# ScalarE as issuer of the projection weights, and a last norm in two VectorE operations with the sample tile first

## The chip, the cores and the metric

The kernel runs on one core of one Trainium2 chip. The core has TensorE (matrix products, here PE), VectorE (DVE), ScalarE (ACT), GpSimd (POOL) and SyncE (SP), each with its own instruction stream, and sixteen DMA engines that SyncE, ScalarE and GpSimd give transfers to. The metric is the device time of one execution in microseconds, lower is better.

## The reference

One inference step of a one-layer decoder for a prompt of 512 rows and 64 sample rows (8 sequences of 8), model width 1024. What matters for the change is the conditioning, the first projection and the last norm:

```python
mod = (jax.nn.silu(c) @ w_ada + b_ada).reshape(B, 6, 1, D_MODEL)
shift1, scale1, gate1, shift2, scale2, gate2 = [mod[:, i] for i in range(6)]
h = x * (1 + scale1) + shift1
proj = h @ w_in                       # 1024 -> 3072: qa, ka, va, qb, kb, vb
...                                   # two kinds of attention, w_o, a first layer norm, ConvFFN up
y = (jax.nn.gelu(a, approximate=False) * g) @ w_down + b_down
x = layer_norm(DEEPNORM_ALPHA * x + gate2 * y, ln2_g, ln2_b)   # (x - mu) * rsqrt(var + EPS) * g + b
```

The step also returns updated window buffers (`win_k_sample`, `win_v_sample`): old cache rows copied from one place of the chip's memory to another, and new rows behind them.

## The kernel before

**First projections.** Work goes in 30 units, numbered n = 5 s + t: section s (0 to 5) is a chunk of 512 columns of `w_in`, t is the row tile (0 to 3 the prompt, t = 4 = TP the sample rows). Every product is made of three float32r products (high by high, high by rest, rest by high; lines 1723 to 1725; for the sample rows of most sections two, lines 1718 and 1719). At the end of a section VectorE and GpSimd split the next chunk into high and rest (lines 1177 to 1180 and 774). Between the units TensorE also makes the later modulation: `ada_rows(ch)` (line 1666) multiplies chunk ch of `w_ada`, which lies in the one buffer `late`, and `ada_sum(ch)` (line 1679) follows one unit later. `LATE_UNIT = {4: 3, 5: 6, 6: 10, 7: 13, 8: 16, 9: 20, 10: 23, 11: 26}` says before which unit: chunk 7 before unit 13, chunk 9 before unit 20. Chunk ch + 1 can be loaded only when the rows of chunk ch are done (`ada_mm`), since both use `late`.

**Who issues what.** Before the change SyncE issues everything in this stage from one list in the order of the units: the stores of projected rows (lines 604 to 625, each behind a wait for the rows), the loads of the next `w_in` chunk (line 544, 2 MB, behind `w_used`), the loads of `late` (line 582, 2 MB, behind `ada_mm`), and the copies of window caches (line 586, `move_window`, 4 MB from memory to memory, at the units of `COPY_UNIT`). A wait for one holds up all that stands behind it. ScalarE copies value rows out of PSUM (line 910) and turned queries (line 916).

**The end.** The down projection has two halves of 512 columns. Half 1 first takes the gated rows f = 0 to 11 for all five tiles, then for one tile after another the last ten, f = 12 to 21: 30 matmuls for a prompt tile, 20 for the sample tile. `split_gated(z)` on VectorE (lines 1533 to 1535) makes the high and rest parts that these read. When a tile is complete VectorE runs `add_half(1, t)` (gate, residual, statistics: lines 1574 to 1578, for the sample tile also 1571 and 1572) and the norm: mean and variance (1626, 1627), a root on ScalarE (1079), reciprocal and factor (1631, 1632), the scaling x * r - mean * r on ScalarE (1074), the product with the norm's weights on VectorE (`weight_norm`, 1620), the addition of its bias on GpSimd (853; for the sample tile on VectorE, 1638), then the store (728, 731). The order of the tiles is 0, 1, 2, 3, TP.

## Time and profile before

| | us |
|---|---|
| median of 3 runs | 1175.63 |
| lowest and highest of them | 1174.1, 1181.54 |
| the profiled execution, its own time | 1176.66 |
| its span in the trace | 1175.0 |
| TensorE busy | 1023.7 (87%) |
| VectorE busy | 827.1 (70%) |

The span is the time from the first to the last record of the trace; the execution's own time is 1.66 us more. The first projections with their modulation lie between 40 and 270 us of the span, attention between 270 and 610, the up projection between 708 and 1060, the down projection and the last norm behind it.

### The profile page before, as it was taken

What the parts mean: (1) busy time and instruction counts of PE and PEld (TensorE: products, weight loads), DVE (VectorE), ACT (ScalarE), POOL (GpSimd) and SP (SyncE); (2) the same over time, 40 slices, a digit from 0 to 9 for tenths busy, and PEclk for the clock granted to TensorE, in tenths of its full rate; (3) what the DMA queues carried; (4) which work ended last, traced back from release to release, by engine and by line L of the source; (5) the groups of instructions that cost most, each with busy time, mean ns of one, the idle gap of its engine ahead of it and who ended that gap; (6) DMA issues with size and microseconds to landing.
All of it is one profiled execution on the core that took longest, in us unless ns stands there. A gap on an engine that the chain in (4) does not pass through costs nothing.

```text
span 1175.0 us, 23900 instructions
## 1 busy us (share of the span) xinstructions
PE 1023.7 (87%) x9297; PEld 832.1 (71%) x9297; DVE 827.1 (70%) x1545; ACT 270.8 (23%) x600; POOL 450.5 (38%) x575
## 2 busy tenths in 40 slices
PE   4599989995788888888888969999999999998994
PEld 2377657673566666566676759999999999776873
DVE  1637545644886877888876784676676767999978
ACT  0300000001343433343352032323232323000001
POOL 0423223214243444434406034565566656333323
PEclk8699999998898989898998988999999999999998
DMA  8948799978899999999963151677676622414102
GB/s 299 410 157 312 269 351 365 318 246 266 289 365 368 327 337 368 349 331 331 337 253 127 42 190 47 219 255 277 248 253 250 215 73 75 155 60 147 53 2 80
DMA packets 101030, 276.54 MB, mean 235 GB/s; under 512 B 9608, under 2 KB 33174, under 8 KB 97317
## 3 DMA queue, kind: packets, MB, share of 16 engines
q1 hardware_dynamic: 85701, 223.56, 54.2%
q0 software_dynamic: 15168, 51.39, 12.6%
q8 instruction: 74, 1.21, 0.4%
q14 instruction: 39, 0.32, 0.1%
q10 hardware_dynamic: 48, 0.05, 0.0%
HBM read 264.60 MB, written 76.69 MB: 290 GB/s over the span
## 4 chain that ended last, share of the span: by engine, by line
PE 53%; DVE 16%; issue 15%; DMA 6%; POOL 5%; SPq 2%; POOLq 2%; ACT 1%; ACTq 0%; DVEq 0%; PEldq 0%
PE wide L1723 15%; PE wide L1724 14%; PE wide L1725 14%; DMA ring<-in_w_ada 2%; DVE ring_r L1180 2%; POOLq L480 1%; PE wide L1666 1%; POOL room L509 1%; DVE ht_r L1533 1%; DMA room<-in_w_ada 1%; DVE ring L1260 1%; POOL x_sb L509 1%; POOL x_sb L805 1%; PE wide L1807 1%; DVE ring_r L1179 1%
## 5 line engine op out<-in xcount | busy, mean ns | idle before, releaser
L828 POOL TENSOR_TENSOR ring_r<-ring,ring_r 128x1024 fp32r<-128x1024 f32 x70 | 180.8, 2592 | 232.3 <-DVE ring_r L1139 201.1
L1723 PE MATMUL wide<-x_sb_r,ring_r 128*128 128x288 f32 x704 | 211.1, 300 | 11.4 <-DVE ht_r L1162 8.4
L1724 PE MATMUL wide<-ht_r,ring_r 128*128 128x288 f32 x704 | 209.3, 297 | 0.0
L1725 PE MATMUL wide<-x_sb_r,ring_r 128*128 128x288 f32 x704 | 208.7, 297 | 0.0
L1723 PEld LDWEIGHTS wide<-x_sb_r,ring_r 128*128 128x128 f32 x704 | 133.4, 190 | 14.3 <-issue 14.3
L1260 DVE STREAM_TRANSPOSE ring<-ring 128x512 f32<-128x512 f32 x208 | 129.0, 677 | 12.0 <-DMA ring<-in_cache_k 10.3
L1725 PEld LDWEIGHTS wide<-x_sb_r,ring_r 128*128 128x128 f32 x704 | 134.2, 191 | 0.0
L1724 PEld LDWEIGHTS wide<-ht_r,ring_r 128*128 128x128 f32 x704 | 133.8, 190 | 0.0
L1723 PE MATMUL wide<-ring_r,x_sb_r 128*128 128x512 f32 (+1 forms) x208 | 87.0, 418 | 11.9 <-DVE ht_r L1162 8.7
L1725 PE MATMUL wide<-ring_r,ht_r 128*128 128x512 f32 x216 | 87.2, 404 | 0.0
L1724 PE MATMUL wide<-ring_r,x_sb_r 128*128 128x512 f32 (+1 forms) x208 | 83.7, 402 | 0.0
L1548 DVE SCALAR_TENSOR_TENSOR room<-room,vec_t 128x512 f32<-128x512 f32 x44 | 55.4, 1260 | 40.0 <-ACT room L1056 40.0
L1048 ACT ACTIVATE room<-wide,vec_t 128x576 f32<-128x576 f32 x44 | 32.8, 744 | 207.1 <-PE wide L1725 202.3
L1725 PE MATMUL wide<-ring_r,room_r 128*128 128x512 f32 x192 | 77.5, 404 | 0.0
L1550 DVE SCALAR_TENSOR_TENSOR room<-room,vec_t 128x512 f32<-128x512 f32 x44 | 73.5, 1671 | 1.6
L774 POOL TENSOR_TENSOR ring_r<-ring,ring_r 128x512 fp32r<-128x512 f32 x24 | 33.5, 1401 | 88.1 <-ACT ring_r L876 44.1
L1139 DVE CAST ring_r<-ring 128x1024 fp32r<-128x1024 f32 x62 | 41.9, 687 | 34.0 <-DMA ring<-in_w_up 32.1
L1807 PE MATMUL wide<-room 128*128 128x128 f32 x320 | 53.9, 303 | 12.0 <-ACT room L950 8.6
L1723 PEld LDWEIGHTS wide<-ring_r,x_sb_r 128*128 128x128 f32 (+1 forms) x208 | 39.9, 192 | 32.6 <-issue 16.7
L517 POOL DMA_DIRECT2D x_sb<-in_cache_v x60 | 33.0, 550 | 72.5 <-issue 71.4
L1723 PE MATMUL wide<-ring_r,ht_r 128*128 128x512 f32 x136 | 55.8, 410 | 5.0 <-DVE room L1574 2.9
L1807 PEld LDWEIGHTS wide<-room 128*128 128x128 f32 x320 | 44.1, 205 | 22.1 <-ACT room L950 12.8
(271 smaller groups left out, 2119.4 us busy)
## 6 DMA issues: line engine op xcount, KB each, us to landing
ring<-in_cache_k SPq DMA_DIRECT2D x128, 256.0 KB
out_wks<-in_cache_win_k SPq DMA_DIRECT2D x8, 4080.0 KB, 19.5
out_wvs<-in_cache_win_v SPq DMA_DIRECT2D x8, 4080.0 KB, 19.3
ring<-in_w_up SPq DMA_DIRECT2D x22, 1024.0 KB, 7.6
room<-in_w_ada SPq DMA_DIRECT2D x8, 2048.0 KB, 9.7
ring<-in_cache_win_k SPq DMA_DIRECT2D x16, 1024.0 KB
x_sb<-in_cache_v POOLq DMA_DIRECT2D x60, 256.0 KB, 5.4
room<-in_cache_v POOLq DMA_DIRECT2D x56, 256.0 KB, 5.3
```

Of the source, the lines that this page charges most:

```text
L517: eng.dma_start(home[t:P:4, :, :], flat_v[1][bass.ds(pg, 1)].rearrange("a (i m) h d -> m (a i) (h d)", i=4))\
L774: nc.gpsimd.tensor_tensor(rest, w, high.bitcast(F32), ALU.subtract).then_inc(win_pool, 1)
L828: nc.gpsimd.tensor_tensor(rest, w, high.bitcast(F32), ALU.subtract).then_inc(wl_rest, 1)
L1048: nc.scalar.activation(u_b[:, k % 2, 2:2 + NT].rearrange("p (h t) -> p h t", h=2), pair, ACT.Identity, bias=vec_t[:, 0, 48 + f:49 + f]).th ...
L1139: nc.vector.tensor_copy(pair_of(n, slice(k, k + 2))[0], slot(SLOT_OF[n])[:, k:k + 2, :]).then_inc(wl_high, 1)
L1260: last = nc.vector.transpose(ktg[:, G % NK, :, 32 * t:32 * t + 32], kraw[G % NK][:, t, :].rearrange("p (g d) -> p g d", d=32))
L1548: then(nc.vector.scalar_tensor_tensor(out=c_p, in0=u_b[:, k % 2, 1:1 + SEQ], scalar=tap(1), in1=c_p, op0=ALU.mult, op1=ALU.add))
L1550: nc.vector.scalar_tensor_tensor(out=c_p, in0=u_b[:, k % 2, 0:SEQ], scalar=tap(0), in1=c_p, op0=ALU.mult, op1=ALU.add)
L1723: nc.tensor.matmul(out, left[0], right[0], start=first, stop=False)
L1724: nc.tensor.matmul(out, left[0], right[1], start=False, stop=False)
L1725: return nc.tensor.matmul(out, left[1], right[0], start=False, stop=last)
L1807: last = nc.tensor.matmul(bank[:, 0:P], pt_b[:, u % 2, P * kb:P * kb + P], vp[:, kb, m, P * (n // 2):P * (n // 2) + P], start=(kb == 0), s ...
```

## The change

1. The function `load_late` moves out of SyncE's part and takes the issuing engine. SyncE still issues chunk 4; chunks 5 to 11 and the `w_in` chunks of sections 2 to 5 are now issued by ScalarE, from its own job list, at positions `at + 0.3` and `n + 0.4` between its copies. The waits in front of them are the same. SyncE keeps stores and window copies.
2. The last norm is two VectorE operations over the whole tile: (x - mean) * weights, which needs no root and runs while ScalarE makes it, and then (that) * r + bias. ScalarE keeps the root alone; GpSimd has no part in it.
3. In half 1 of the down projection the last ten f of the sample tile come first: `END_TILES = [TP, 0, 1, 2, 3]`. VectorE, ScalarE and the stores follow that order.

```diff
+        END_TILES = [TP, 0, 1, 2, 3]
...
+        def load_late(eng, ch):
+            if ch > 4:
+                eng.wait_ge(ada_mm, ch)
+            src = a["w_ada"][0].rearrange("(k p) n -> p k n", p=P)
+            eng.dma_start(late, src[:, :, CH * ch:CH * ch + CH]).then_inc(late_in, 16)
...
@@ SyncE, at the end of each unit
-                if t == TP:
-                    if s < 4:
-                        load_chunk(6 + s)
-                for ch, at in LATE_UNIT.items():
-                    if at == n and ch < 11:
-                        load_late(ch + 1)
...
@@ ScalarE, the projections
+            jobs += [(at + 0.3, "late", ch + 1) for ch, at in LATE_UNIT.items() if ch < 11]
+            jobs += [(n + 0.4, "w_in", 2 + s) for n, (s, t) in enumerate(units) if t == TP and s < 4]
             for _, what, n in sorted(jobs):
+                if what == "late":
+                    load_late(act, n)
+                    continue
+                if what == "w_in":
+                    c = CHUNK_AT[("in", n)]
+                    act.wait_ge(w_used, chunk_before(c) + 1)
+                    act.dma_start(slot(SLOT_OF[c]), src_in[:, :, CH * n:CH * n + CH]).then_inc(w_in_slot[SLOT_OF[c]], 16)
+                    continue
...
@@ ScalarE, the last norm
-                nc.scalar.activation(x, x, ACT.Identity, bias=mv2[0:rows, t, 4:5], scale=mv2[0:rows, t, 3:4]).then_inc(n2_scaled, 1)
...
@@ GpSimd
-            for t in range(TP):
-                pool.wait_ge(n2_w, t + 1)
-                nc.gpsimd.tensor_tensor(x_sb[:, t, :], x_sb[:, t, :], ln2[:, 2, :], ALU.add).then_inc(y_out, 1)
...
@@ VectorE, the last norm
-            for t in range(TP + 1):
+            for i, t in enumerate(END_TILES):
                 add_half(1, t)
...
                 nc.vector.tensor_scalar(v[:, 1:2], v[:, 1:2], EPS, None, ALU.add).then_inc(n2_var, 1)
-                if 0 < t < TP:
-                    weight_norm(t - 1)
-                dve.wait_ge(n2_rt, t + 1)
+                nc.vector.scalar_tensor_tensor(out=x, in0=x, scalar=v[:, 0:1], in1=ln2[0:rows, 1, :],
+                                               op0=ALU.subtract, op1=ALU.mult)
+                dve.wait_ge(n2_rt, i + 1)
                 then(nc.vector.reciprocal(v[:, 3:4], v[:, 2:3]))
-                nc.vector.scalar_tensor_tensor(out=v[:, 4:5], in0=v[:, 0:1], scalar=-1.0, in1=v[:, 3:4],
-                                               op0=ALU.mult, op1=ALU.mult).then_inc(n2_fac, 1)
+                nc.vector.scalar_tensor_tensor(out=x, in0=x, scalar=v[:, 3:4], in1=ln2[0:rows, 2, :],
+                                               op0=ALU.mult, op1=ALU.add).then_inc(y_out, 1)
...
@@ TensorE, half 1 of the down projection
-                    steps += [(f, t) for t in range(TP + 1) for f in range(TAIL, FT)]
+                    steps += [(f, t) for t in END_TILES for f in range(TAIL, FT)]
```

On SyncE, from the first window copy of the projections on (`out_wks` and `out_wvs` behind `<-in_cache_win` are the copies, `in_w_ada` the loads of `late`), before:

```order
L586 DMA out_wks<-in_cache_win_k 64x16320
L582 DMA room<-in_w_ada 128x8x512 [waits ada_product]
L544 DMA ring<-in_w_in 128x8x512 [waits w_used]
L586 DMA out_wvs<-in_cache_win_v 64x16320
L604 DMA out_wkp<-mix 128x512 [waits rope_done] x2
L582 DMA room<-in_w_ada 128x8x512 [waits ada_product]
L604 DMA out_wkp<-mix 128x512 [waits rope_done] x2
L586 DMA out_wks<-in_cache_win_k 64x16320
L608 DMA out_wks<-ring 8x512 [waits rope_done]
L608 DMA out_wks<-ring 8x512 x7
L544 DMA ring<-in_w_in 128x8x512 [waits w_used]
L619 DMA out_wvp<-room 128x512 [waits proj_taken_act]
```

And with the change, from the same copy on:

```order
L585 DMA out_wks<-in_cache_win_k 64x16320
L585 DMA out_wvs<-in_cache_win_v 64x16320
L603 DMA out_wkp<-mix 128x512 [waits rope_done] x4
L585 DMA out_wks<-in_cache_win_k 64x16320
L607 DMA out_wks<-ring 8x512 [waits rope_done]
L607 DMA out_wks<-ring 8x512 x7
L618 DMA out_wvp<-room 128x512 [waits proj_taken_act] x2
```

The loads are gone from between the stores, and two copies stand next to each other (the same happens at the third pair, units 14 and 18).

On ScalarE, from the first turned queries (unit 0) to the first transfers of attention, before:

```order
L916 ACTIVATE room<-wide 128x4x128 [waits qk_transposed] x4
L910 ACTIVATE room<-wide 128x512 [waits proj_product] x4
L910 ACTIVATE ring<-wide 64x512 [waits proj_product]
L916 ACTIVATE room<-wide 128x4x128 [waits qk_transposed] x4
L910 ACTIVATE room<-wide 128x512 [waits proj_product] x4
L910 ACTIVATE ring<-wide 64x512 [waits proj_product]
```

And with the change, the first part of the same stretch (to unit 14):

```order
L915 ACTIVATE room<-wide 128x4x128 [waits qk_transposed]
L526 DMA room<-in_w_ada 128x8x512 [waits ada_product]
L915 ACTIVATE room<-wide 128x4x128 [waits qk_transposed]
L902 DMA ring<-in_w_in 128x8x512 [waits w_used]
L915 ACTIVATE room<-wide 128x4x128 [waits qk_transposed] x2
L526 DMA room<-in_w_ada 128x8x512 [waits ada_product]
L902 DMA ring<-in_w_in 128x8x512 [waits w_used]
L909 ACTIVATE room<-wide 128x512 [waits proj_product]
L526 DMA room<-in_w_ada 128x8x512 [waits ada_product]
L909 ACTIVATE room<-wide 128x512 [waits proj_product] x3
L526 DMA room<-in_w_ada 128x8x512 [waits ada_product]
L909 ACTIVATE ring<-wide 64x512 [waits proj_product]
```

Chunk 7 is the `in_w_ada` row between the first value copy (unit 10) and the next three.

On VectorE, the last tile of the program, before (the sample tile, with the weights of tile 3 and the bias behind it):

```order
L1571 COPY room<-wide 64x512 [waits down_product]
L1572 TENSOR_TENSOR room<-room,wide 64x512 [waits dve_seq]
L1574 TENSOR_TENSOR room<-room,mix 64x512 [waits dve_seq]
L1577 TENSOR_TENSOR x_sb<-x_sb,room 64x512 [waits down_taken]
L1578 BN_STATS stat<-x_sb 64x6 [waits dve_seq]
L1626 BN_AGGR mv<-stat 64x2 [waits dve_seq]
L1627 TENSOR_SCALAR mv<-mv 64x1 [waits dve_seq]
L1631 RECIPROCAL mv<-mv 64x1 [waits norm2_root]
L1632 SCALAR_TENSOR_TENSOR mv<-mv 64x1 [waits dve_seq]
L1620 TENSOR_TENSOR x_sb<-x_sb,room 128x1024 [waits norm2_scaled]
L1620 TENSOR_TENSOR x_sb<-x_sb,room 64x1024 [waits norm2_scaled]
L1638 TENSOR_TENSOR x_sb<-x_sb,room 64x1024 [waits norm2_weighted]
```

And with the change (prompt tile 3 is now the last):

```order
L1567 TENSOR_TENSOR room<-wide,mix 128x512 [waits down_product]
L1570 TENSOR_TENSOR x_sb<-x_sb,room 128x512 [waits down_taken]
L1571 BN_STATS stat<-x_sb 128x6 [waits dve_seq]
L1613 BN_AGGR mv<-stat 128x2 [waits dve_seq]
L1614 TENSOR_SCALAR mv<-mv 128x1 [waits dve_seq]
L1615 SCALAR_TENSOR_TENSOR x_sb<-x_sb,mv,room 128x1024
L1618 RECIPROCAL mv<-mv 128x1 [waits norm2_root]
L1619 SCALAR_TENSOR_TENSOR x_sb<-x_sb,mv,room 128x1024 [waits dve_seq]
```

Twelve instructions behind the last product have become eight, and no wait for ScalarE's scaling is among them.

## Rows read from the trace of the kernel before

**Rows 1.** The page: busy us, share of the span, instructions, of TensorE.

```profile
PE 1023.7 (87%) x9297; PEld 832.1 (71%) x9297; DVE 827.1 (70%) x1545; ACT 270.8 (23%) x600; POOL 450.5 (38%) x575
```

**Rows 2.** Timeline of TensorE, 117 to 200 us: start, us, engine, line, operation, [idle before].

```profile
122.76 1.90 PE L1666 MATMUL wide<-room,c_t 128*9 128x512 f32 x16
...
150.58 3.18 PE L1666 MATMUL wide<-room,c_t 128*9 128x512 f32 x16 [3.65 <-DMA room<-in_w_ada]
153.69 0.80 PE L1723 MATMUL wide<-ring_r,x_sb_r 128*128 128x512 f32 x1
...
197.48 1.90 PE L1666 MATMUL wide<-room,c_t 128*9 128x512 f32 x16
```

**Rows 3.** Timeline of the transfers that SyncE issues, 10 to 292 us.

```profile
120.77 0.52 SPq L586 DMA_DIRECT2D out_wks<-in_cache_win_k  x1
...
136.67 0.41 SPq L544 DMA_DIRECT2D ring<-in_w_in  x1
...
137.74 0.43 SPq L582 DMA_DIRECT2D room<-in_w_ada  x1
...
174.42 0.40 SPq L582 DMA_DIRECT2D room<-in_w_ada  x1
174.86 10.52 SPq L586 DMA_DIRECT2D out_wvs<-in_cache_win_v  x1
```

**Rows 4.** Transfers issued at 120.8, 137.7 and 174 to 175: KB, us to landing.

```profile
out_wks<-in_cache_win_k SPq DMA_DIRECT2D x1, 4080.0 KB, 15.4
...
room<-in_w_ada SPq DMA_DIRECT2D x1, 2048.0 KB, 12.8
...
out_wvs<-in_cache_win_v SPq DMA_DIRECT2D x1, 4080.0 KB, 32.0
room<-in_w_ada SPq DMA_DIRECT2D x1, 2048.0 KB, 21.0
```

**Rows 5.** Timeline of ScalarE: the value copy of unit 10, and turned queries later.

```profile
130.96 0.60 ACT L910 ACTIVATE room<-wide 128x512 f32<-128x512 f32 x1 [33.08 <-PE wide L1725]
...
186.89 0.60 ACT L916 ACTIVATE room<-wide 128x512 f32<-128x512 f32 x1 [20.10 <-PE wide L1783]
```

**Rows 6.** Two stretches: us, busy us by engine, granted clock, DMA share, GB/s.

```profile
70.00:80.00 10.00, 10.00 (x55) 6.98 (x54) 3.40 (x7) 0.60 (x1) 2.57 (x2) 1.00 0.11 19
150.00:160.00 10.00, 9.42 (x45) 5.68 (x45) 0.69 (x1) 0.17 (x1) 0.00 (x0) 0.83 1.19 431
```

**Rows 7.** Timeline of TensorE and VectorE in half 1 of the down projection.

```profile
1129.30 0.50 PE L1723 MATMUL wide<-ring_r,room_r 128*128 128x512 f32 x1 [2.43 <-DVE room_r L1535]
...
1134.06 0.43 PE L1725 MATMUL wide<-ring_r,room_r 128*128 128x512 f32 x1
...
1132.25 0.69 DVE L1535 TENSOR_TENSOR room_r<-room,room_r 128x512 fp32r<-128x512 f32 x1
...
1159.16 0.40 PE L1719 MATMUL wide<-ring_r,room_r 128*64 128x512 f32 x1
```

**Rows 8.** Timeline of VectorE behind the last prompt tile, to the end.

```profile
1154.97 0.69 DVE L1574 TENSOR_TENSOR room<-wide,mix 128x512 f32<-128x512 f32 x1 [0.60 <-PE wide L1725]
...
1157.46 1.22 DVE L1620 TENSOR_TENSOR x_sb<-x_sb,room 128x1024 f32<-128x1024 f32 x1
1158.59 0.16 DVE L1631 RECIPROCAL mv<-mv 128x1 f32<-128x1 f32 x1
1158.78 2.34 DVE L1632 SCALAR_TENSOR_TENSOR mv<-mv 128x1 f32<-128x1 f32 x1
...
1170.40 1.22 DVE L1638 TENSOR_TENSOR x_sb<-x_sb,room 64x1024 f32<-64x1024 f32 x1
```

**Rows 9.** Line 1511, a scalar-tensor-tensor over a tile: ns min/median/max, first and last start.

```profile
L1511 DVE SCALAR_TENSOR_TENSOR x_sb<-x_sb,room x5: 1207/1215/1216, 641.3 to 688.9; 128x1024 f32<-128x1024 f32 x4, 64x1024 f32<-64x1024 f32 x1
```

**Rows 10.** The last stores: issue on SyncE, and KB and us to landing.

```profile
1171.65 0.53 SPq L731 DMA_DIRECT2D out_ys<-x_sb  x1
...
out_yp<-x_sb SPq DMA_DIRECT2D x4, 512.0 KB, 2.6
```

More of the change, by code:

```diff
@@ L380, in build @@
         g_used = sem("gated_used")
-        n2_var, n2_rt, n2_fac = sem("norm2_variance"), sem("norm2_root"), sem("norm2_factors")
-        n2_scaled, n2_w = sem("norm2_scaled"), sem("norm2_weighted")
-        y_last = sem("y_sample_ready")
+        n2_var, n2_rt = sem("norm2_variance"), sem("norm2_root")
         st_done = sem("sample_tile_of_h2")
@@ L574, in _ @@
             sp.dma_start(pages[:, :], a["page_table"].rearrange("b n -> (b n)").rearrange("(o n) -> o n", o=1)).then_inc(page_in, 16)
-            def load_late(ch):
-                if ch > 4:
-                    sp.wait_ge(ada_mm, ch)
-                src = a["w_ada"][0].rearrange("(k p) n -> p k n", p=P)
-                sp.dma_start(late, src[:, :, CH * ch:CH * ch + CH]).then_inc(late_in, 16)
             def move_window(i, names=(("cache_win_k", "wks"), ("cache_win_v", "wvs"))):
@@ L590, in flat @@
                 return ap.rearrange("t h d -> t (h d)")
-            load_late(4)
+            load_late(sp, 4)
             n_rope = n_v = 0
@@ L903, in _ @@
                     jobs.append((n + 2.5, "q", n))
+            jobs += [(at + 0.3, "late", ch + 1) for ch, at in LATE_UNIT.items() if ch < 11]
+            jobs += [(n + 0.4, "w_in", 2 + s) for n, (s, t) in enumerate(units) if t == TP and s < 4]
+            src_in = a["w_in"][0].rearrange("(k p) n -> p k n", p=P)
             for _, what, n in sorted(jobs):
+                if what == "late":
[6 more added lines that the diff above has]
+                    continue
                 s, t = units[n]
@@ L1068, in _ @@
                 nc.scalar.activation(conv_out(i), bk(6 + i % 2)[0:18, :], ACT.Copy).then_inc(us_a, 1)
-            def scale_norm(t):
+            for i, t in enumerate(END_TILES):
                 rows = P if t < TP else NS
-                act.wait_ge(n2_fac, t + 1)
-                x = x_sb[0:rows, t, :]
-                nc.scalar.activation(x, x, ACT.Identity, bias=mv2[0:rows, t, 4:5], scale=mv2[0:rows, t, 3:4]).then_inc(n2_scaled, 1)
-            for t in range(TP + 1):
-                rows = P if t < TP else NS
-                act.wait_ge(n2_var, t + 1)
+                act.wait_ge(n2_var, i + 1)
                 nc.scalar.activation(mv2[0:rows, t, 2:3], mv2[0:rows, t, 1:2], ACT.Sqrt).then_inc(n2_rt, 1)
-                scale_norm(t)
         @block.vector
@@ L1567, in add_half @@
                 j = (TP + 1) * half + t
-                dve.wait_ge(dn_mm, j + 1)
+                done = (TP + 1) * half + (END_TILES.index(t) if half else t) + 1
+                dve.wait_ge(dn_mm, done)
                 src = bk(j % 8)[0:rows]
@@ L1574, in add_half @@
                 nc.vector.tensor_tensor(y3[0:rows], src, gate2[0:rows, kind, cols], ALU.mult).then_inc(dn_d, 1)
-                dve.wait_ge(dn_d, j + 1)
+                dve.wait_ge(dn_d, done)
                 x = x_sb[0:rows, t, cols]
@@ L1614, in _ @@
                     add_half(0, z - FT - NG_BUF + 2)
-            def weight_norm(t):
-                rows = P if t < TP else NS
-                x = x_sb[0:rows, t, :]
-                dve.wait_ge(n2_scaled, t + 1)
-                nc.vector.tensor_tensor(x, x, ln2[0:rows, 1, :], ALU.mult).then_inc(n2_w, 1)
-            for t in range(TP + 1):
+            for i, t in enumerate(END_TILES):
                 rows = P if t < TP else NS
@@ L2103, in _ @@
                     z, j = FT * half + f, (TP + 1) * half + t
-                    if t == 0:
+                    if t == (END_TILES[0] if half and f >= TAIL else 0):
                         if half == 0 and f == 10:
```

9 lines of the change are left out of this document (2 added, 7 removed).

## The prediction

> **What bounds the kernel now.** I read the page first: TensorE is busy for 1023.7 us of a span of 1175.0 [rows 1]. So a change elsewhere can pay only where TensorE waits, or in front of its first and behind its last matmul. This change touches two such places.
>
> The first is the projections. I listed TensorE's idle times in its timeline from 60 to 270 us. There is one wait of over 2 us: 3.65 us in front of the rows of chunk 7, released by the DMA of `in_w_ada` [rows 2]. SyncE's list shows why that load is late [rows 3]. It is issued at 137.74, though its condition (rows of chunk 6 done, begun at 122.76 [rows 2]) held at about 124.6. In front of it stand the window stores, which wait for the rotary rows of unit 9, and the load of the `w_in` chunk of section 3, issued at 136.67. It lands after 12.8 us, at 150.5 [rows 4], and TensorE starts at 150.58. The other waits of this stretch are under 2 us, and none is for a DMA. The short ones belong to VectorE's and GpSimd's splits and stay.
>
> The second is the end. The last matmul starts at 1159.16 and takes 0.40 [rows 7], so 15.4 us follow to the end of the span. In them VectorE finishes tile 3's norm, does the sample tile, the two `weight_norm` and the bias, to 1171.62 [rows 8], and the last store takes the rest [rows 10]. Among those operations is one of a single column (line 1632) that took 2.34 us [rows 8], while GpSimd added a bias in the same time.
>
> **The projections, part by part.** ScalarE issues chunk 7 behind its value copy of unit 10, which runs from 130.96 to 131.56 [rows 5]. That is about 131.6 in place of 137.74, 6.1 us earlier. The `w_in` chunk of section 3 waits for the product of unit 9, which TensorE finishes just before the rows of chunk 6 at 122.76 [rows 2], so it goes 14 us earlier, from 136.67 [rows 3] to about 122.6. Chunk 7 now shares the DMA engines with the end of the window copy of 120.77, which took 15.4 us to land [rows 4], and with that `w_in` chunk. Where it lands is bounded from both sides. With its 12.8 us of before [rows 4], when it had the `w_in` chunk in front of it too, it lands at 144.4. In the worst case the copy is served first (to 136.2), and then both chunks in the 13.9 us from 136.67 to 150.5 [rows 3, 4], which gives 150.1. TensorE needs it at 150.58 - 3.65 = 146.9. The worst case puts all of `w_in` behind the copy, although it is issued only 1.8 us after it and has 9 us alone with it, so I take the first: the wait goes, whole.
>
> What goes with it is read in the rows: 3.65 us of wait; the sixteen matmul records behind it took 3.18 us, where the same sixteen took 1.90 at 122.76, so 1.28 more: from 150 to 160 us the granted clock was 0.83 of full speed [rows 6], part of it at 1.2 GHz in place of 2.4, right behind the idle time; and the next one took 0.80 [rows 2], about 0.3 more than after a full-speed group. Sum 3.65 + 1.28 + 0.3 = 5.2 us. Bounds: 0.5 (worst landing) and 5.2.
>
> The other six late loads move by little, since their condition sets them: chunk 5 with the rows of chunk 4, chunk 8 behind the value copy of unit 13, as before. The issue itself costs ScalarE about 0.4 us each by SyncE's rows [rows 3], eleven times, beside 23% busy [rows 1]: on no path. What the waits in front of them hold up are ScalarE's copies of the next unit, which come later than the condition anyway. SyncE, freed of its waits, sends two copies close together twice. The first pair goes out at about 50 us, in front of a stretch in which the DMA engines had little to do (share 0.11 from 70 to 80 us [rows 6]) and nothing waits for a load. The second goes out behind unit 14, and that is the place to watch (first rival).
>
> Attention starts with loads issued behind the last value copy, so it moves up whole. Nothing in it has a fixed time, so I carry the 5.2 us to the end.
>
> **The end, part by part.** TensorE gets later. The splits of f = 18 to 21 are what it waits for in the first of the five tiles (2.43 us idle at 1129.30); the last one is done at 1132.94 [rows 7]. Before, prompt tile 0 stood there with 30 matmuls, ending at 1134.3. Now the sample tile stands there with two matmuls per f: the last pair starts at 1133.0 and issues in 0.86 at the half clock (0.43 each at 1134.06 [rows 7]), to 1133.9. Behind it come 120 matmuls of prompt tiles in place of 90 and the sample tile's 20, at 0.228 apiece (110 from 1134.06 to 1159.16 [rows 7], so 6.8 us per tile). The last starts at 1133.9 + 119 x 0.228 = 1161.0 and ends at 1161.4, where it was 1159.56: 1.8 us later. If the half clock lasts 3 us longer, because TensorE has less to do under the splits, 1.5 more.
>
> VectorE: from the end of a prompt tile to the start of the first big operation it takes 1157.46 - 1154.97 = 2.49 us [rows 8]. The two big ones are not in this trace in this form. Nearest above and below in kind are line 1511, a scalar-tensor-tensor over 128x1024, at 1.215 us [rows 9], and line 1620, a tensor-tensor of that size, at 1.22 [rows 8]; with a pointer to a column as scalar I see no reason for more or less, and take 1.22 each (bounds 1.2 and 1.4). The reciprocal begins 1.13 behind the first, the second 0.19 behind that [rows 8]. The root on ScalarE is done within the first. Sum per prompt tile: 2.49 + 1.13 + 0.19 + 1.22 = 5.0 us, under the 6.8 that TensorE needs per tile. So VectorE waits for TensorE at each, and only one tile's 5.0 stands behind the last matmul. The sample tile needs about 6.4 us (two more operations of 0.7), from 1133.9 to 1140.3, just before tile 0 at 1140.7.
>
> The end is then 1161.4 + 5.0 + the store. The sample store took 1175.0 - 1171.65 = 3.35 from issue to the end; a prompt tile's store lands after 2.6 [rows 10], so between 2.6 and 3.35, and I take 3.25, since it is the last one's case. With 0.04 to VectorE's start, 1161.4 + 0.04 + 5.03 + 3.25 = 1169.7 in place of 1175.0: gain 5.3 us, bounds 3.5 (long half clock, dearer operations) and 6.0 (landing 2.6).
>
> **Sum.** 5.2 + 5.3 = 10.5 us. The profiled execution's own time was 1176.66, which gives 1166.2. It lay 1.03 above the median of 1175.63, which gives 1165.1. I predict 1165.
>
> **Rivals.** *Copies crowd out the loads.* Chunk 9 landed at 174.42 + 21.0 = 195.4 [rows 3, 4], with only 2.1 us to spare before its rows at 197.48 [rows 2]. Now it is on another engine's queue beside two window copies; the second was issued at 174.86 and landed 32.0 later, at 206.9 [rows 3, 4]. If a load of small rows is served behind copies of large ones, it lands when they do. All of this moves 5.2 earlier: the deadline to 192.3 and the second copy's landing to 201.7 at the latest, so the wait is up to 9.4 us, and I take about half, 5. For it: the thin margin. Against it: chunk 9 is 2 MB, and if the engines give each queue half of their time it is through before either copy, since it then needs no more than twice the 5 to 6 us that 2 MB take alone (chunk 7 landed 13.9 us behind the issue of 4 MB). With 5 us of wait and 1.5 of half clock (1.28 + 0.3 above) the projections' gain is gone: 1165.0 + 6.5 = 1171.5.
>
> By the Trainium skill ("DMA: Bandwidth & Descriptors", "Queues, rings and completion order") each DMA engine goes round-robin between the queues of SyncE and ScalarE, packet by packet; by that the load is not starved, unless a copy's packets are much the larger. No row of before has a copy beside ScalarE's loads, so the trace is silent on it.
>
> *The load lands no earlier.* The DMA engines move the same bytes, and if chunk 7 comes at 150.1 as in the worst case above, 0.5 of the 5.2 remains: 1169.7. For it: copy, `w_in` and chunk 7 are 8 MB from 120.8 on. The Trainium skill ("DMA: Bandwidth & Descriptors", "Issuing engines are not separate DMA queues") says that issuing from several engines saves only the time of issue, which speaks for this one; the row of the wait shows that here the time of issue is the point, since the load stood 13 us behind its condition.
>
> *Slower than before.* Starvation at every load: if those before units 13, 16, 20, 23 and 26 each came late by as much as chunk 7 does now, each would cost 5.2. It decides from the third such wait: none gained, two more lost, 1175.63 - 5.3 + 10.4 = 1180.7. Against it: only chunk 9 has a copy on both sides, and ScalarE's queue copies have slack (one of them waits 20.10 us at 186.89 [rows 5]).
>
> **Chances.** Forecast, 1162.5 to 1167.5: 0.62. Crowding, 1168 to 1173: 0.20. Lands no earlier, 1167.5 to 1170.5: 0.09. Slower, about 1180: 0.03. More than forecast, since clock and splits fall otherwise: 0.06. The range 1161.5 to 1172 leaves out 0.03 below, the slower case and part of the crowding. One per cent of this time, 11.8 us, is about what a measurement can tell: 1163.9 is the border. The forecast lies just above it; a third of its chance and the larger gain fall below: faster 0.26, same 0.71, slower 0.03.
>
> **What would show it.** Right: no wait of TensorE for `in_w_ada` at unit 13, chunk 7 issued near 131.6, unit 13's rows near 147; chunk 9's rows without a wait; the end of attention 5 us earlier. In the tail the last matmul about 1.8 us later against the end of the splits, two VectorE operations of 1.2 us per tile, 8.3 us between the last matmul and the end. Wrong: a wait before unit 20, big operations of 2 us or more, or a half clock that lasts into tile 1.

## The result: slower, by two waits of TensorE for late loads

| | before | after |
|---|---|---|
| median of 20 runs each, us | 1174.63 | 1186.86 |
| lowest and highest | 1167.53, 1181.54 | 1171.48, 1194.21 |
| the profiled execution, its own time | 1176.66 | 1189.11 |
| its span | 1175.0 | 1187.4 |

The ratio is 1.0066, 95% interval 1.0043 to 1.009. It leaves out runs over 1.5% above the fastest of their kernel, as a disturbed run would be; the times after spread more widely than that by themselves, so that the medians, 12.2 us or 1.0% apart, say it better. The twenty times fall in two groups: four from 1171.5 to 1176.9 and sixteen from 1181.2 to 1194.2. The profiled execution is of the second group.

In the kernel after, matmul lines 1723 to 1725 are 1705 to 1707, the late load is line 526, the load of `w_in` 902, a window copy 585 and `ada_rows` 1648. The first view is what TensorE waits for from 40 to 285 us. The columns are the line that waits, its releaser, us in total, times, and the longest.

```profile
PE wide L1648 <- DMA room<-in_w_ada: 21.9, 2, 14.2
```

TensorE's timeline shows where these two stand (start, us, engine, line, [idle before]). They answer to the wait of 3.65 us in [rows 2].

```profile
161.63 3.60 PE L1648 MATMUL wide<-room,c_t 128*9 128x512 f32 x16 [14.16 <-DMA room<-in_w_ada]
...
217.07 3.60 PE L1648 MATMUL wide<-room,c_t 128*9 128x512 f32 x16 [7.78 <-DMA room<-in_w_ada]
```

The first is unit 13 (chunk 7), the second unit 20 (chunk 9). Now the two queues side by side. ScalarE's timeline, its DMA issues:

```profile
122.55 0.37 ACTq L902 DMA_DIRECT2D ring<-in_w_in  x1
...
131.51 0.38 ACTq L526 DMA_DIRECT2D room<-in_w_ada  x1
...
178.16 0.37 ACTq L902 DMA_DIRECT2D ring<-in_w_in  x1
...
186.13 0.37 ACTq L526 DMA_DIRECT2D room<-in_w_ada  x1
```

SyncE's timeline, the copies:

```profile
121.30 0.52 SPq L585 DMA_DIRECT2D out_wks<-in_cache_win_k  x1
143.09 0.52 SPq L585 DMA_DIRECT2D out_wvs<-in_cache_win_v  x1
181.61 0.52 SPq L585 DMA_DIRECT2D out_wks<-in_cache_win_k  x1
182.17 0.59 SPq L585 DMA_DIRECT2D out_wvs<-in_cache_win_v  x1
```

Chunk 7 and the `w_in` chunk of section 3 are issued when I said they would be, 131.5 and 122.6. But the view of the DMA gives 30.1 us from issue to landing for chunk 7, in place of 12.8 [rows 4], and 21.4 for the `w_in` chunk ahead of it:

```profile
ring<-in_w_in ACTq DMA_DIRECT2D x1, 2048.0 KB, 21.4
...
room<-in_w_ada ACTq DMA_DIRECT2D x1, 2048.0 KB, 30.1
```

What the engines did in the meantime is in the rows by queue (q1 is SyncE's, q10 ScalarE's; packets, MB, share of sixteen engines, which passes 100% where the times of packets overlap). From 123 to 130 us, copy of 121.30 and `w_in` together:

```profile
q1 hardware_dynamic: 32, 2.09, 87.2%
q10 hardware_dynamic: 16, 0.03, 1.6%
```

From 148 to 157 us, copy of 143.09 and chunk 7; and from 186.5 to 198 us, the copies of 181.61 and 182.17 and the two loads of 178.16 and 186.13, which land after 33.3 and 30.9 us:

```profile
q1 hardware_dynamic: 52, 3.26, 99.0%
q10 hardware_dynamic: 44, 0.09, 2.6%
...
q1 hardware_dynamic: 80, 4.18, 102.7%
q10 hardware_dynamic: 71, 0.14, 3.5%
```

And from 211 to 217 us, when both copies are through:

```profile
q10 hardware_dynamic: 1134, 2.29, 103.3%
```

A packet of a load is about 2 KB, one of a copy 65 KB (2.09 MB in 32; of the 80 packets of 186.5 to 198 us, 65 are of over 8 KB). The engines go between the queues in packets, so beside a copy a load gets about a thirtieth of the bytes, as 2 KB are of 65; alone it moves 2 MB in under 6 us. So each 4 MB copy takes nearly all of the engines and the load waits for its end. That is the chain: `w_in` waits for the copy of 121.30 (landed at 137.1) and lands at 144.0; chunk 7 comes behind it in ScalarE's queue; and just then, at 143.09, SyncE sends the next copy, which lands 17.2 us later. Its packets fill the engines from about 147.5 us on. By 148 chunk 7 has all but 0.25 of its 2.1 MB, and for this last eighth it needs until 161.6. In the kernel before, that copy was issued after chunk 7 on the same queue, and so could not pass it.

The Trainium skill says ("DMA: Bandwidth & Descriptors", "Queues, rings and completion order") that each engine goes round-robin between the queues packet by packet. The trace agrees where both queues have work for the whole stretch: 52 packets to 44 from 148 to 157 us, and 80 to 71 from 186.5 to 198. The first stretch, with 32 to 16, begins before the load's packets do; from 128 to 134 us it is 32 to 32.

The projections end later by this. A good mark is the first load of window keys for attention on SyncE, at 270.02 before and at 287.32 after: 17.3 us. The two waits are 21.94 us against 3.65 before, 18.3 more. From the mark to the end it is 1187.4 - 287.3 = 900.1 us against 905.0.

The end itself came out nearly as drawn up. VectorE's timeline, the last prompt tile's norm, answers to [rows 8]:

```profile
1181.69 1.27 DVE L1615 SCALAR_TENSOR_TENSOR x_sb<-x_sb,mv,room 128x1024 f32<-128x1024 f32 x1
1182.89 0.15 DVE L1618 RECIPROCAL mv<-mv 128x1 f32<-128x1 f32 x1
1183.08 1.28 DVE L1619 SCALAR_TENSOR_TENSOR x_sb<-x_sb,mv,room 128x1024 f32<-128x1024 f32 x1
```

The last matmul starts at 1178.77 and ends at 1179.16, 8.2 us ahead of the end of the span. The place that answers to the head of [rows 7] is, in TensorE's timeline:

```profile
1145.95 0.67 PE L1700 MATMUL wide<-ring_r,room_r 128*128 128x512 f32 x1 [3.12 <-DVE room_r L1527]
```

From there to the end of the span it is 41.4 us; before it was 1175.0 - 1129.3 = 45.7. One part is not as drawn up. The last matmul starts 32.8 us behind that row (1178.77 - 1145.95), where it was 29.9 (1159.16 - 1129.30), so it is 3.0 us later and not 1.8.

### The profile page after: what moved, and what is told of

It reads as the page before. It is cut to its first block, busy times and chain, and to the rows that moved or that the text cites. A ratio compares the mean times of both kernels' runs of the same rounds, so it can differ in the third digit from the quotient of the medians.

```text
span 1187.4 us, 23890 instructions
## 1 busy us (share of the span) xinstructions
PE 1025.9 (86%) x9297; PEld 831.9 (70%) x9297; DVE 819.1 (69%) x1544; ACT 264.5 (22%) x595; POOL 442.6 (37%) x571
## 2 busy tenths in 40 slices
DMA packets 101030, 276.54 MB, mean 233 GB/s; under 512 B 9608, under 2 KB 33174, under 8 KB 97317
## 4 chain that ended last, share of the span: by engine, by line
PE 47%; DVE 19%; issue 15%; DMA 9%; POOL 5%; POOLq 2%; SPq 1%; ACT 1%; ACTq 0%; DVEq 0%; PEldq 0%
PE wide L1705 13%; PE wide L1706 13%; PE wide L1707 13%; DMA room<-in_w_ada 5%; DVE ht_r L1525 2%; DMA ring<-in_w_ada 2%; PE wide L1648 2%; DVE ring_r L1172 2%; POOLq L479 2%; DVE ht_r L1526 1%; DVE room_r L1527 1%; POOL room L508 1%; PE wide L1845 1%; DVE x_sb L1601 1%; DVE ring_r L1131 1%
## 5 line engine op out<-in xcount | busy, mean ns | idle before, releaser
L1705 PE MATMUL wide<-ring_r,x_sb_r 128*128 128x512 f32 (+1 forms) x208 | 86.9, 418 | 13.6 <-DVE ht_r L1154 10.6
L1707 PE MATMUL wide<-ring_r,ht_r 128*128 128x512 f32 x216 | 86.7, 401 | 0.0
L1540 DVE SCALAR_TENSOR_TENSOR room<-room,vec_t 128x512 f32<-128x512 f32 x44 | 52.6, 1196 | 42.0 <-ACT room L1055 42.0
L1542 DVE SCALAR_TENSOR_TENSOR room<-room,vec_t 128x512 f32<-128x512 f32 x44 | 73.5, 1671 | 1.6
L1131 DVE CAST ring_r<-ring 128x1024 fp32r<-128x1024 f32 x62 | 42.0, 688 | 32.8 <-DMA ring<-in_w_up 31.0
L1845 PE MATMUL wide<-ring,x_sb 128*32 128x128 f32 (+1 forms) x1792 | 59.8, 279 | 3.2 <-DVE ring L1252 2.7
```

Of the source, the lines that this page charges most:

```text
L1131: nc.vector.tensor_copy(pair_of(n, slice(k, k + 2))[0], slot(SLOT_OF[n])[:, k:k + 2, :]).then_inc(wl_high, 1)
L1540: then(nc.vector.scalar_tensor_tensor(out=c_p, in0=u_b[:, k % 2, 1:1 + SEQ], scalar=tap(1), in1=c_p, op0=ALU.mult, op1=ALU.add))
L1542: nc.vector.scalar_tensor_tensor(out=c_p, in0=u_b[:, k % 2, 0:SEQ], scalar=tap(0), in1=c_p, op0=ALU.mult, op1=ALU.add)
L1705: nc.tensor.matmul(out, left[0], right[0], start=first, stop=False)
L1707: return nc.tensor.matmul(out, left[1], right[0], start=False, stop=last)
L1845: last = nc.tensor.matmul(bank[32 * nn:32 * nn + 32, at:at + nk], qbd[:, w % 2, g].rearrange("p i q -> p (i q)"), keys[:, g, 0:nk], start= ...
```

## Experiments

Twelve kernels were run, 4 to 12 times each, and each beside the kernel before on the same chip. As between the kernels above, single profiles differ by several us from attention on, so the verdicts rest on the ratios of repeated runs and on where waits stand. I call the mark of the last section (the first load of window keys) "the mark"; it is 270.0 before and 287.3 after. Chunk 4, loaded ahead of anything that the experiments move, is issued between 45.7 and 48.9 us, so marks that differ by 1 or 2 us say little.

My theory (A): the loss is all in the projections, because loads of small rows on one queue meet copies of large rows on the other; the end gains what it was to gain.

### 1. Each half of the change alone

`tail_only` has the new norm and order of tiles and all loads on SyncE as before. `issue_only` has the loads on ScalarE and the norm of before.

> The second and third part of the change alone (two VectorE operations for the last norm, the sample tile first); SyncE issues all loads as before. If the loss of the whole change lies in the projections, this one gains: from the end of the splits to the end of the span 37.8 us as in the changed kernel, in place of 42.1, so about 4.3 us faster than before, near 1170. If the tail has a part in the loss, this one is no faster than 1174.

> The first part of the change alone: ScalarE issues the loads of the first projections, the last norm as before. Theory (window copies crowd out the loads on ScalarE's queue): TensorE waits for chunks 7 and 9, as in the changed kernel by 14 and 8 us in place of 3.65, so 15 to 17 us slower than before where it falls as it did in the profiled execution, about 1188 to 1192, with a wide spread. Rival (the loss comes with the tail): about 1170.

| | median | ratio, 95% interval |
|---|---|---|
| tail_only | 1172.82 | 0.9956 (0.9934 to 0.9977) |
| issue_only | 1191.69 | 1.0137 (1.0081 to 1.0193) |

The end gains 0.44% of 1177.6, 5.2 us. The issue by ScalarE loses over 1%, in the range expected. The profiled execution of `issue_only` was the fastest of its four (1179.91, the others 1190.7 to 1198.3), and shows how narrow the edge between the two groups of times probably is. There the `w_in` chunk landed at 142.9, chunk 7 began, and the copy of unit 11 was issued at 144.19, 1.3 us behind the landing: chunk 7 landed after 17.8 us and TensorE waited 0.26. In the profile of the change the copy was issued 0.9 us ahead of the landing (143.09 and 144.0), and the wait was 14.16. These are two profiles, one of each kernel; what the other executions did at this place no trace shows. Unit 20 waited all the same, in TensorE's timeline of `issue_only`:

```profile
202.16 3.42 PE L1671 MATMUL wide<-room,c_t 128*9 128x512 f32 x16 [7.96 <-DMA room<-in_w_ada]
```

### 2. Small rows in the copies

`small_rows` is the changed kernel, but each of the eight copies of the projections goes as two transfers, of the even and of the odd rows of 2 KB.

```diff
-                    sp.dma_start(o[dst][0, i, 0:PAST - DS], a[name][0, i, DS:PAST]).then_inc(copied, 16)
+                    if i < 4:
+                        for odd in range(2):
+                            sp.dma_start(o[dst][0, i, odd:PAST - DS:2], a[name][0, i, DS + odd:PAST:2]).then_inc(copied, 16)
```

> The changed kernel, but the eight window copies of the projections go as even and odd rows of 2 KB each, the same bytes in the same places of SyncE's list. Theory A (a DMA engine takes one descriptor of each queue in turn, so a copy with descriptors of up to 65 KB gets nearly all of the time beside rows of 2 KB): the loads now get about half, chunk 7 lands before 147 us and chunk 9 before 192, no wait, 1163 to 1167. Theory B (SyncE's queue goes first, or the bandwidth is simply not there): waits as in the changed kernel, near 1187.

Measured: 1170.6 us, ratio 0.9929 (0.9898 to 0.9959). One wait for `in_w_ada` is left at unit 13, where I had expected none (chunk 7 lands at 148.1), and none at unit 20:

```profile
148.14 1.91 PE L1652 MATMUL wide<-room,c_t 128*9 128x512 f32 x16 [2.79 <-DMA room<-in_w_ada]
```

The DMA by queue from 123 to 137 us, copy beside `w_in`:

```profile
q1 hardware_dynamic: 1427, 2.89, 56.6%
q10 hardware_dynamic: 1175, 2.38, 46.3%
```

With packets of one size the two queues share nearly evenly; from 125 to 135 us, when both are busy throughout, it is 913 packets to 942 and 1.84 MB to 1.93. The same bytes move, the same engines issue them at the same places, and what was 1% slower is 0.7% faster. The size of the packets is the cause, and theory B is out. The mark is at 266.0. Beside the end alone (`tail_only`, 0.9956) the gain is small, and the intervals overlap: the early loads still share the engines with the copies.

### 3. Without the copies

`no_copies` leaves out the eight window copies of the projections (their rows of the output are not written).

> The changed kernel without the eight window copies of the projections (33 MB, those output rows are left out; the other eight stay). Theory A and B alike (the loads wait because of the copies): each load lands in 7 to 9 us, no wait for in_w_ada, about 1163 to 1165. Rival C (a load issued by ScalarE is slow by itself, or its issue is late): waits before units 13 and 20 stay at several us.

Measured: 1166.81 us, ratio 0.9908 (0.9878 to 0.9939). No wait for the late loads is left, and those that ScalarE issues land in 7.8 to 9.0 us, one, issued 2.7 us behind a `w_in` chunk, in 10.6. The mark is at 266.4. Rival C, that ScalarE's issue is slow by itself, is out.

`no_copy_11` leaves out only the copy of 143.09 (its rows of the output are not written).

```diff
+                    if i == 1 and dst == "wvs":
+                        sp.sem_inc(copied, 16)
+                        continue
```

> The changed kernel without one of its copies: the window copy of unit 11 (the second sample's values) is left out, so that part of wvs is not written. Theory A (that copy, issued at 143.09, took chunk 7's bandwidth): chunk 7 lands at 142 to 150, PE waits 0 to 3 us for it in place of 14.2, and the two groups of times (1171 to 1177, and 1181 to 1194) become one; the wait of unit 20 (7.8 us) stays; the time is 1172 to 1177 us, a ratio of 0.995 to 1.0. Rival D (the w_in load ahead of it on its own queue holds chunk 7 back): the wait stays above 8 us and the time above 1181 us.

Measured: 1174.83 us, ratio 0.9989 (0.9964 to 1.0014). Nine of its ten times lie between 1170.5 and 1176.9, one is 1182.4. Chunk 7 landed after 17.9 us, at 149.0, and TensorE waited 1.96 us for it and 8.7 at unit 20. So this one copy makes the slow group, and rival D, under which the `w_in` chunk was enough, is out.

### 4. The queues exchanged

`copies_on_act` leaves the loads with SyncE and gives ScalarE the copies.

```diff
+            jobs += [(n + 0.35, "copy", n) for n in COPY_UNIT]
...
+                if what == "copy":
+                    i, which = COPY_UNIT[n]
+                    name, dst = ("cache_win_k", "wks") if which == "k" else ("cache_win_v", "wvs")
+                    act.wait_ge(pj_mm, n + 1)
+                    act.dma_start(o[dst][0, i, 0:PAST - DS], a[name][0, i, DS:PAST]).then_inc(copied, 16)
```

> The two queues are exchanged: the late loads and the w_in loads stay on SyncE's queue as before, and the eight window copies of the projections are issued by ScalarE, each behind the matmuls of the unit at which it stood. The last norm is that of the changed kernel. Theory A (the DMA engines take the two queues by turns, one packet each, and a packet of a 4 MB copy is ten times longer and more than one of a load): it doesn't matter which engine issues what, and the loads starve as in the changed kernel: chunk 7, issued at about 137.7, lands at 155 to 165, and PE waits 8 to 16 us for it; the time is 1180 us or more, a ratio of 1.005 to 1.02. Rival B (SyncE's queue is served ahead of ScalarE's): the loads land as fast as they do alone, in 8 to 13 us, there is no wait above 4 us, and the time is that of the tail change alone or less, 1165 to 1173 us, a ratio of 0.990 to 0.996.

Measured: 1199.64 us, ratio 1.0244 (1.0184 to 1.0304). The waits, in TensorE's timeline:

```profile
163.22 3.60 PE L1647 MATMUL wide<-room,c_t 128*9 128x512 f32 x16 [13.99 <-DMA room<-in_w_ada]
...
268.50 3.60 PE L1647 MATMUL wide<-room,c_t 128*9 128x512 f32 x16 [11.00 <-DMA room<-in_w_ada]
```

and the DMA by queue from 148 to 158 us, with the copy, now in q10, fully under way:

```profile
q10 hardware_dynamic: 48, 3.13, 87.0%
q1 hardware_dynamic: 48, 0.10, 2.6%
```

Rival B is out: neither queue goes first. It is the copy that wins, whoever issues it, and the turns are one packet for one, 48 to 48. (A stretch that begins earlier hides this: from 146 to 148 us the load, still almost alone, moves 348 packets.) The mark is at 297.5. The time is above the range that I gave. Of the 10 us between the marks the waits for `in_w_ada` make 3.1 (25.0 us in all). The rest is in TensorE's own busy time: 213.8 us from 40 to 298 in place of 206.0 from 40 to 287, for nearly the same number of matmul records (988 and 985), with a granted clock of 0.88 in place of 0.90.

### 5. One queue, loads ahead of the stores

`sp_early` has SyncE issue everything, with each load ahead of the stores of its unit, and one copy a unit later.

```diff
-COPY_UNIT = {..., 8: (1, "k"), ...}
+COPY_UNIT = {..., 9: (1, "k"), ...}
...
+                if t == TP and s < 4:
+                    load_chunk(6 + s)
+                for ch, at in LATE_UNIT.items():
+                    if at == n + 1 and ch < 11:
+                        load_late(ch + 1)
                 kb_rows = slice(P * t, P * t + P)
```

> One queue, but the loads ahead: SyncE issues everything, as before, but each w_in and late load is issued ahead of the stores of its unit, and not behind them, and the copy of unit 8 stands one unit later. The last norm is that of the changed kernel. Theory A (what costs is two queues with packets of such unequal size, and the early issue is worth its full wait where the queue is one): the wait of 3.7 us for chunk 7 becomes 0 to 1.5 us, unit 20 doesn't wait, and the time is 1163 to 1170 us, a ratio of 0.988 to 0.994. Rival C (an early load always meets a copy, on either queue): the copy ahead of it in the queue delays chunk 7 as much as the issue gains, the wait stays at 3 to 5 us, and the time is that of the tail change alone, about 1172 us, a ratio of 0.995 to 0.998.

Measured: 1174.29 us, ratio 0.9981 (0.9958 to 1.0004), no better than the end alone (0.9956). My expectation of 1163 to 1170 was missed, and the DMA rows say why. Chunk 7 is issued at 125.36 and lands after 11.7 us, so unit 13 waits for nothing. But the copies of 137.34 and 143.22 now go out together, and chunk 8, issued at 149.49, stands behind them and lands after 24.2 us:

```profile
173.75 3.60 PE L1642 MATMUL wide<-room,c_t 128*9 128x512 f32 x16 [5.87 <-DMA room<-in_w_ada]
```

The rival C of this run was right in what it said of an early load, one load later than I put it. These copies and loads landed in the order of their issue, and with 8 MB in front of it the load took 24.2 us, where 7.8 to 9.0 were enough in `no_copies`.

### 6. The copies moved to the second half

`late_copies_act` is the changed kernel with its eight copies moved out of the projections. `late_copies_sp` is the same with the loads on SyncE as before.

```diff
-                if n in COPY_UNIT:
-                    i, which = COPY_UNIT[n]
-                    move_window(i, (("cache_win_k", "wks") if which == "k" else ("cache_win_v", "wvs"),))
...
+            move_window(0)
             load_chunk(FIRST_LATE + 13)
+            move_window(1, (("cache_win_k", "wks"),))
...
             for n in range(FIRST_LATE + 17, len(CHUNKS)):
                 load_chunk(n)
+                if n == FIRST_LATE + 17:
+                    move_window(1, (("cache_win_v", "wvs"),))
+                    move_window(2)
+                elif n == FIRST_LATE + 18:
+                    move_window(3)
```

> The changed kernel, with nothing left out, but its eight window copies of the projections are issued by SyncE in the second half of the program: three around the load of 944 to 971 us, three behind the load of 1077, two behind the load of 1110, where the page's rows show the DMA engines idle for over half of the time. Theory A (the copies beside the early loads are the whole loss, and the early issue is worth 3.7 to 4 us once they are gone): no wait for in_w_ada is above 1 us, the projections end 3.5 to 4 us earlier than in the kernel before, and the time is 1164 to 1169 us, a ratio of 0.989 to 0.993, near that of the kernel without these copies (0.9908). Rival E (the copies meet later loads or stores just as badly): a new wait of 3 us or more for in_w_up, in_w_down or the spilled rows after 900 us, and a ratio of 0.994 or more.

> The same move of the copies, but with the loads issued by SyncE behind the stores as in the kernel before (the last norm is that of the changed kernel). It tells what the issue by ScalarE is worth by itself once no copy is near. Chunk 7 is then issued at about 137.7 and lands 8 to 9 us later, at about 146.5, so that its wait is 0 to 1 us in place of 3.7: if so, the time is within 1.5 us of that of the other kernel with late copies, 0.989 to 0.994, and ScalarE's queue isn't needed at all. If the issue by ScalarE is worth more than that, this kernel is 3 us or more behind the other.

| | median | ratio, 95% interval | the mark | wait at unit 13 |
|---|---|---|---|---|
| late_copies_act | 1179.35 | 1.0033 (1.0014 to 1.0053) | 264.2 | none |
| late_copies_sp | 1184.61 | 1.0066 (1.0041 to 1.0092) | 270.9 | 3.85 |

Two things follow. First, the early issue is worth what the prediction put on it: with no copy near, the kernel with ScalarE's issue is 5.3 us faster by the medians (the means are 5.1 apart, 95% interval about 2 to 8). Its mark is 6.7 us earlier, of which 1.3 was there at the issue of chunk 4 (46.48 against 47.83), so 5.4 are of the projections. My expectation that SyncE's issue would do as well was wrong. It is late by its place behind the stores and behind the `w_in` chunk: `w_in` goes at 137.43, chunk 7 at 138.50, and it lands after 13.0 us even without a copy.

Second, rival E holds for this placement, by my own fault. TensorE's timeline of `late_copies_act` has, in place of 1.80 and 2.43 us in the kernel before:

```profile
1000.13 0.80 PE L1710 MATMUL wide<-ring_r,ht_r 128*128 128x512 f32 x1 [6.76 <-DVE ht_r L1532]
...
1131.17 0.77 PE L1705 MATMUL wide<-ring_r,room_r 128*128 128x512 f32 x1 [5.63 <-POOL ring_r L825]
```

The second is plain: SyncE's list has three copies behind the load of 1077.76, and the last load of `w_down` at 1110.95; it landed after 16.6 us, against 6.8 before, and GpSimd began its split at 1128.31, 16.78 us idle. The first comes about in the same way: the chunk of `w_down` issued at 965.93, behind two copies and with one right after it, lands after 13.7 us, against 8.1 before, and VectorE, which splits it, waits 7.68 us for it at 979.70, against 1.15. The DMA engines looked idle on the page because the next load was not due yet, and a copy that takes them 11 us fits such a gap only if nothing stands behind it. The same two waits stand in `late_copies_sp` (6.25 and 6.05 us), so the comparison of the two is fair.

### 7. The norm and the order apart

`norm_only` is `tail_only` with the sample tile last, as before. `order_only` is the kernel before with the sample tile first.

> The kernel before with the two-operation last norm, but the sample tile last in its part as before. If the gain of the end is all from the norm (the sample tile's place worth nothing): 1169 to 1174 us, a ratio of 0.993 to 0.998, as with the whole change of the end (0.9956). If the sample tile's place gives a part, as I reckoned (the last tile, one of 128 rows, has a longer store but the sample tile's fixed wait for its matmuls is earlier): about 1175 us, a ratio of 0.998 to 1.0.

> The kernel before with its last norm on three engines as it is, but the sample tile first in its part. Beside the kernel with the two-operation norm alone (0.9946), which left the order, it splits the end's gain of about 5 us. By my reckoning of the prediction the order is worth little: the last tile is then a full one, with a store of 2.6 us, as the tile before it had: a ratio of 0.997 to 1.001. If the order carries the gain: 0.993 to 0.996.

| | median | ratio, 95% interval | first wait of half 1's last part to the end, us |
|---|---|---|---|
| norm_only | 1167.84 | 0.9946 (0.9923 to 0.9968) | 1166.1 - 1125.5 = 40.6 |
| order_only | 1177.27 | 1.0010 (0.9992 to 1.0027) | 1179.3 - 1131.6 = 47.7 |
| tail_only | 1172.82 | 0.9956 (0.9934 to 0.9977) | 1177.0 - 1135.6 = 41.4 |
| before | | | 1175.0 - 1129.3 = 45.7 |

The norm is the whole gain, and no gain of the order shows: by the last column, which is of single profiles, the order costs 0.8 us with the new norm and 2.0 with the old. It leaves TensorE the sample tile's few matmuls, where the splits set the pace, with the long tiles still to come. From the end of the last split to the start of the last matmul it is 26.2 us before and 26.1 in `norm_only`, but 29.2 to 29.6 in `tail_only`, `order_only` and the changed kernel, which have the sample tile first. The ratios alone can't tell what the order costs; the intervals overlap.

### 8. Two copies moved to where no load follows

`two_late` is the changed kernel with the two copies of units 11 and 18 behind the last load of `w_down`.

```diff
-COPY_UNIT = {..., 8: (1, "k"), 11: (1, "v"), 14: (2, "k"), 18: (2, "v"), ...}
+COPY_UNIT = {..., 8: (1, "k"), 14: (2, "k"), ...}
...
             for n in range(FIRST_LATE + 17, len(CHUNKS)):
                 load_chunk(n)
+            for i in (1, 2):
+                move_window(i, (("cache_win_v", "wvs"),))
```

> The changed kernel, nothing left out, with two of the eight window copies of the projections (those of units 11 and 18, which stand beside chunks 7 and 9) issued by SyncE behind the last load of w_down, at about 1105 to 1110 us, where nothing is loaded any more. Unlike the kernel with eight late copies no load stands behind them. Theory A (only a copy in the way of a load costs): the waits for in_w_ada are 0 to 3 us at unit 13 and 0 to 2 us at unit 20, the last w_down chunk lands in 4 to 9 us (16.6 behind three copies), VectorE's and GpSimd's splits of it wait for nothing new, and the time is 1166 to 1171 us, a ratio of 0.991 to 0.996, which beats both kernels and comes near that of small rows (0.9929). Rival F (8 MB of copies beside the end of the down projection and its stores costs by itself, for instance by the chunk's own landing): the end from the last issue of w_down on is 3 us or more longer than in the changed kernel, and the ratio is 0.997 or more.

Measured: 1166.79 us, ratio 0.9916 (0.9888 to 0.9943), faster than the kernel before and than the changed one with nothing left out, and within the error of the kernel without copies. It can't be told apart from `norm_only` (0.9946), which has SyncE issue everything: the intervals overlap. Unit 13's wait is 1.69 us, unit 20 has none, the last `w_down` chunk lands after 7.0:

```profile
150.89 1.90 PE L1650 MATMUL wide<-room,c_t 128*9 128x512 f32 x16 [1.69 <-DMA room<-in_w_ada]
...
1129.20 0.50 PE L1702 MATMUL wide<-ring_r,room_r 128*128 128x512 f32 x1 [3.12 <-DVE room_r L1529]
```

From the second row to the end it is 41.9 us, half a microsecond more than in the changed kernel, so rival F, in which copies beside the end cost 3 us or more, is out.

## Why the prediction was wrong

**The sign was wrong**, and the range did not hold the time: 1165 (1161.5 to 1172) against 1186.86. The term for the end nearly held, the one for the projections did not.

- *When the loads are issued.* "About 131.6" and "about 122.6": 131.51 and 122.55. Right.
- *Where chunk 7 lands.* This is the step that failed. I bounded it between 144.4 and 150.1 and took 144.4, at which the whole wait of 3.65 us goes; it landed at 161.6, and the wait was 14.16. The worst case had the copy of 120.77 served first, then both loads. It lacked the copy of unit 11. Before, that copy stands on SyncE's queue at 142.5, behind the load of 137.74, and can't pass it; I listed what chunk 7 would be moved past on SyncE's list, but not what would now be beside it in the time in which it moves its bytes. Taking that copy away brings the wait from 14.16 to 1.96 us, with chunk 7 at 149.0: inside my bounds, but near the worst one, so that even then the value that I took was wrong.
- *How the engines share.* I argued for my value that `w_in` has 9 us alone with the copy of 120.77, and against crowding that the load "is through before either copy", "if the engines give each queue half of their time". They give turns in packets, one for one, and in bytes that was 2.09 MB to 0.03 in seven of the 9 us on which I built. The sentence on the Trainium skill had the right rule with its exception, "unless a copy's packets are much the larger", and then called the trace silent on it; but that some packets are large could have been read from the page of the kernel before, which counts 101030 packets, of them 97317 under 8 KB. With equal packets the forecast's mechanism works in part: the wait falls to 2.79 us, not to nothing (0.9929).
- *What the early issue is worth once the bytes come.* 5.2 us: 5.3 in medians between the kernels with late copies. Right, but shown only there.
- *The end.* 5.3 us, bounds 3.5 to 6.0: 5.2 by `tail_only` and 4.3 by the trace (45.7 to 41.4). The operations took 1.27 and 1.28 for 1.22; from the last matmul to the end 8.2 us for 8.3. What was off is TensorE's part: its last matmul came 3.0 us later for 1.8, since the half clock lasted longer, the case that I had kept for the bound (matmuls are 0.43 us apart until 1152.8, 3.2 us behind the last split; before, until 1134.1, 1.1 behind it). Right as a sum. The splitting of it was not: moving the sample tile, which I carried as part of one schedule, costs 0.8 to 2.0 us by single profiles, and the norm gives over 5.
- *The rivals.* Crowding was the right mechanism at chunk 9, priced at 5 us and 1171.5. The wait there was 7.78, inside the 9.4 that I had as its upper bound, and I halved it. It was missed at chunk 7, with 14.2. "Slower than before" was the outcome; its price of 5.2 a wait and its "third such wait" were mis-sized: two waits with 18.3 us more in all sufficed. With the right price, 1175.63 - 5.3 + 18.3 = 1188.6.
- *The chances.* 0.20 and 0.03 for the two starvation cases were too low for a term of which the text itself said that no row showed it. The two profiles of unit 13 show the same: with the copy issued 0.9 us ahead of a landing the wait was 14.16 us, with 1.3 behind it 0.26. *The load lands no earlier*, at 0.09, is about what `no_copy_11` gave: chunk 7 at 149.0 for 150.1.

What stays open: whether the edge read from two profiles explains each run of the two groups, and what the early issue adds in a kernel that leaves nothing out and keeps its copies, since `two_late` and `norm_only` can't be told apart.

## What to carry to other kernels

Before a load is given a queue of its own, list what is in flight on the other queues from its issue to its landing, with the size of each one's packets: a queue served in order, which delays the load, may also be what keeps a large copy behind it. If large copies between places of memory must run beside loads that something waits for, cut them into rows of the loads' size, or put them where no load follows. An edit with two independent halves is to be costed, and tried, half by half.

## What the runs showed of the hardware

- Two queues that both had work got turns of about one packet each, whatever the packets' size: 48 to 48, 44 to 52, 71 to 80, and with 2 KB rows on both 942 to 913. Beside a copy with packets of 65 KB, 2 KB rows on the other queue so got 0.09 MB against 3.26 in 9 us, and 0.14 against 4.18 in 11.5; with 2 KB rows on both, 2.38 against 2.89 in 14. It is the same with the issuing engines exchanged (0.10 against 3.13 in 10 us).
- A copy of 4 MB from memory to memory in rows of 2 KB cost the kernel as a whole no more than in large packets (1170.6 us against 1186.9 with the same loads on the other queue).
- A scalar-tensor-tensor over 128x1024 with a column pointer as scalar took 1.27 to 1.29 us, and 1.26 to 1.28 over 64 rows. One over a single column took 2.33 to 2.38 us while GpSimd added a bias (2.35 to 2.40 us), and 0.15 to 0.16 with GpSimd idle, as at the first tile of the kernel before.
